# Latent attention with scores formed keys by queries, and row maxima from a separate product

## The chip, the cores and the metric

The kernel runs on one core of one Trainium2 chip. The metric is the device time of one execution in microseconds (us). It is one decoder layer on 1024 tokens with 1024 features; inputs, weights and output are float32.

## What is computed

Each layer normalizes the residual, projects it, and runs two attention branches whose gated sum is projected back; an MLP and an embedding step follow. The change is in branch B, the multi-head latent attention: 8 heads, a 64-wide part without position and a 32-wide rotary part in query and key, values 64 wide, causal.

```python
def _mla_attention(q, k, v):   # q, k (B,S,8,64+32); v (B,S,8,64)
    logits = jnp.einsum('bqhd,bshd->bhqs', qb, k).astype(jnp.float32) * scale
    logits = jnp.where(causal, logits, -jnp.inf)
    probs = jax.nn.softmax(logits, axis=-1).astype(v.dtype)
    o = jnp.einsum('bhqs,bshd->bqhd', probs, v)
```

## The kernel before, in words

The program is written by hand for five instruction streams: `pe` (TensorE), `dve` (VectorE), `act` (ScalarE), `pool` (GpSimd) and `sp` (a DMA queue). Each runs its own list in order, and they meet only in semaphores. Most matmuls take operands that were split into a high part and a low part of type fp32r, and sum three products (high by high, high by low, low by high). A few take plain float32.

After the gate projections (which end at about 388 us) comes a preparation for branch B: `q_nope` and the key products (L2423) fill PSUM, ScalarE writes the high parts (`qn_hi` L1361, `kn_hi` L1373), VectorE the low parts (`qn_lo` L1824, `kn_lo` L1835), rotates the rotary parts (`rope`, L1806 to L1808, L1830, L1852), and scales the keys by their inverse norm (`kn`, L1857). The inverse norm of a query is applied later, as a factor of the exponential. `latent_values` (L2485) forms the values; their first group is copied by ScalarE (L1377), the second by ScalarE (L1385) and VectorE (L1870).

Attention is a list `STEPS` of 64 steps, 32 of branch B, then 32 of branch A. A step is a tile of 128 queries (number i) and a pair p of heads (e = 0, 1). The two heads of a pair lie on partitions 0 to 63 and 64 to 127, so their two score matmuls use different rows of TensorE's array. Steps alternate long and short tiles. In step n of branch B:

- `scores_b(n)` (L2507 and L2511): for each chunk of up to 512 keys, five terms for both heads, the 128 queries as stationary operand and the keys as moving one. Result: queries on partitions, keys along the row, in banks 4 to 7.
- VectorE subtracts the causal mask and takes each row's maximum in one instruction (L1921), scales it (L1923), and raises `shift_ready`. `scores_b(n+1)` waits for it.
- ScalarE applies the exponential with that shift and sums each row at the same time (L1430).
- `turn_probs` (L2544): TensorE transposes each 128x128 tile of the probabilities into a ring of three banks, and ScalarE (L1394) and VectorE (L1882) copy it to SBUF.
- `sum_values` (L2558): float32 matmuls, the values as stationary operand of 64 columns, 128 queries moving, both heads of the pair in different columns of the array. ScalarE copies the result (L1413).

The row sums of branch B are inverted, transposed and spread over partitions during branch A (`invert_sums`, `turn_inverse`, `spread_inverse`, `scale_y`, L1886 to L1899). ScalarE and VectorE split the keys and queries of branch A (L1435, L1933, L1439, L1938) at fixed steps. GpSimd forms low parts of weights (`lo_parts`, L1037) and is otherwise idle in branch B. Branch A (`scores_a`, L2528) has the same pipeline, with a mask of its own; then come the output projections (L2282 and others), the MLP (L2677, L2718) and the rest.

## Time and profile before

| what | value |
|---|---|
| median of 3 runs | 1649.94 us (1649.73 to 1650.37) |
| the profiled execution, its own time | 1650.06 us |
| its span (first to last instruction) | 1648.3 us |
| TensorE's mean granted clock | 0.996 |
| TensorE busy | 1596.7 us (97%) |
| VectorE, ScalarE, GpSimd busy | 1201.2, 699.9, 637.1 us |

Times in the profile count from the start of the span. The busy time is the union of the instructions of an engine; the number in parentheses is the share of the span. PE is TensorE's matmuls and PEld its weight loads. DVE is VectorE, ACT is ScalarE, POOL is GpSimd. A matmul's duration is longer than the distance to the next one, since they overlap; so costs of TensorE are read from the starts.

### The profile page before, as it was taken

Reading aid. Unit: us, or ns where it says so; the run is one execution under the profiler, and the core shown is the slowest. Engines: PE = TensorE matmul, PEld = TensorE weight load, DVE = VectorE, ACT = ScalarE, POOL = GpSimd, SP = SyncE. Lnnn points to the kernel's source line nnn. Section 1 sums busy time; section 2 is a strip of 40 time slices with the busy share of each in tenths; the row PEclk is TensorE's granted clock in tenths of the full one; section 3 lists DMA queues with packets and bytes.
Section 4 is the critical chain, followed back from the end, with each engine's and each line's share of the span. In section 5 each row is a group of like instructions: output and inputs, shape, how many; then the busy total and the mean of one; then the engine's idle time right before and its main releaser. Section 6 shows DMA issues by size and latency. Waiting matters only on the chain.

```text
span 1648.3 us, 23187 instructions
## 1 busy us (share of the span) xinstructions
PE 1596.7 (97%) x8576; PEld 1296.1 (79%) x8576; DVE 1201.2 (73%) x1851; ACT 699.9 (42%) x1151; POOL 637.1 (39%) x397
## 2 busy tenths in 40 slices
PE   6999999999999999999999999999999999999997
PEld 5778888787777777778888788888878888888786
DVE  7679999982656677754354777776699999898445
ACT  5432422323566677621144443343354444444223
POOL 2222532213200002012213545445589888885230
PEclk9999999999999999999999999999999999999999
DMA  5312223243300010203442354555494544422112
GB/s 164 93 39 58 96 77 102 90 126 82 90 1 2 1 40 2 78 25 131 168 137 89 119 169 141 160 171 160 155 338 170 204 163 166 141 90 64 45 58 102
DMA packets 115240, 177.46 MB, mean 108 GB/s; under 512 B 19104, under 2 KB 73376, under 8 KB 115008
## 3 DMA queue, kind: packets, MB, share of 16 engines
q1 hardware_dynamic: 111296, 162.44, 30.2%
q10 hardware_dynamic: 3680, 13.63, 2.2%
q8 instruction: 64, 1.05, 0.3%
q14 instruction: 40, 0.33, 0.1%
q0 software_dynamic: 160, 0.02, 0.0%
HBM read 123.24 MB, written 49.68 MB: 105 GB/s over the span
## 4 chain that ended last, share of the span: by engine, by line
PE 87%; DVE 7%; ACT 3%; issue 2%; POOL 1%; DMA 1%; SPq 0%; ACTq 0%; DVEq 0%
PE ps L2282 35%; PE ps L2718 18%; PE ps L2677 17%; PE ps L2544 3%; PE ps L2558 2%; PE ps L2507 2%; PE ps L2528 2%; PE ps L2423 2%; DVE prob_a L1921 1%; PE ps L2362 1%; PE ps L2330 1%; DVE prob_b L1921 1%; PE ps L2511 1%; PE ps L2641 1%; PE ps L2384 1%
## 5 line engine op out<-in xcount | busy, mean ns | idle before, releaser
L1037 POOL TENSOR_TENSOR w_lo<-w_raw,w_hi 128x1024 fp32r<-128x1024 f32 x67 | 166.1, 2480 | 481.9 <-ACT w_hi L1187 481.9
L1106 POOL TENSOR_TENSOR a_lo<-s_raw,a_hi 128x512 fp32r<-128x512 f32 x128 | 189.8, 1490 | 95.2 <-ACT a_hi L1466 94.8
L1187 ACT ACTIVATE w_hi<-w_raw 128x1024 fp32r<-128x1024 f32 x67 | 70.9, 1059 | 343.0 <-PE ps L2282 275.3
L2677 PE MATMUL ps<-b_hi,a_hi 128*128 128x512 f32 x448 | 175.3, 391 | 3.7 <-POOL a_lo L1106 1.7
L2718 PE MATMUL ps<-b_hi,a_hi 128*128 128x512 f32 x448 | 174.5, 390 | 2.4 <-DVE h L2155 2.4
L2677 PE MATMUL ps<-b_hi,a_lo 128*128 128x512 f32 x448 | 174.4, 389 | 0.0
L2677 PE MATMUL ps<-b_lo,a_hi 128*128 128x512 f32 x448 | 174.3, 389 | 0.0
L1106 POOL TENSOR_TENSOR a_lo<-f_raw,a_hi 128x512 fp32r<-128x512 f32 x96 | 136.8, 1439 | 97.1 <-ACT a_hi L1466 97.0
L2718 PE MATMUL ps<-b_lo,a_hi 128*128 128x512 f32 x448 | 174.3, 389 | 0.0
L2718 PE MATMUL ps<-b_hi,a_lo 128*128 128x512 f32 x448 | 174.3, 389 | 0.0
L2282 PE MATMUL ps<-n_hi,w_hi 128*128 128x512 f32 x544 | 168.3, 391 | 2.4 <-ACT rel L1247 1.3
L1769 DVE TENSOR_SCALAR_CACHE_REDUCE tested<-sc,bar_i 128x384 bf16<-128x384 f32 (+2 forms) x192 | 169.0, 942 | 1.7 <-POOL sc L1052 0.6
L2282 PE MATMUL ps<-n_hi,w_lo 128*128 128x512 f32 x544 | 167.5, 389 | 0.0
L2282 PE MATMUL ps<-n_lo,w_hi 128*128 128x512 f32 x544 | 167.4, 389 | 0.0
L2155 DVE TENSOR_TENSOR h<-h,ps 128x512 f32<-128x512 f32 x224 | 142.8, 677 | 23.4 <-PE ps L2718 23.0
L2105 DVE TENSOR_TENSOR b_lo<-b_lo,b_hi 128x512 fp32r<-128x512 f32 x112 | 143.5, 1321 | 0.1
L2282 PEld LDWEIGHTS ps<-n_hi,w_hi 128*128 128x128 f32 x544 | 101.8, 188 | 25.2 <-ACT rel L1247 1.7
L2282 PEld LDWEIGHTS ps<-n_lo,w_hi 128*128 128x128 f32 x544 | 102.1, 188 | 21.2
L2282 PEld LDWEIGHTS ps<-n_hi,w_lo 128*128 128x128 f32 x544 | 102.1, 188 | 21.2
L1466 ACT ACTIVATE a_hi<-s_raw 128x512 fp32r<-128x512 f32 x128 | 78.7, 627 | 92.5 <-PE ps L2718 90.9
L2677 PEld LDWEIGHTS ps<-b_hi,a_hi 128*128 128x128 f32 x448 | 84.1, 188 | 23.3 <-POOL a_lo L1106 3.3
L2718 PEld LDWEIGHTS ps<-b_hi,a_hi 128*128 128x128 f32 x448 | 84.1, 188 | 21.0 <-issue 3.5
(356 smaller groups left out, 3224.4 us busy)
## 6 DMA issues: line engine op xcount, KB each, us to landing
f_raw<-in_w_ff_dram SPq DMA_DIRECT2D x64, 512.0 KB, 4.3
b_lo<-hid_scratch SPq DMA_DIRECT2D x112, 256.0 KB, 5.5
hid_scratch<-c_out SPq DMA_DIRECT2D x32, 512.0 KB, 3.7
w_raw<-in_w_in_dram SPq DMA_DIRECT2D x28, 512.0 KB, 3.7
hid_scratch<-t_out SPq DMA_DIRECT2D x15, 768.0 KB, 6.1
...
```

What stands on the lines that cost most here:

```text
L1037: pool.tensor_tensor(lo_of(first)[:, :, :], w_raw[s][:, :, :], hi_of(first)[:, :, :].bitcast(F32), ALU.subtract).then_inc(lo_ready, 1)
L1106: pool.tensor_tensor(slot(a_lo, o), first_of(o), slot(a_hi, o).bitcast(F32), ALU.subtract).then_inc(a_lo_done, 1)
L1187: act.activation(hi_of(first)[:, :, :], w_raw[s][:, :, :], ACT.Copy).then_inc(hi_ready, 1)
L1466: act.activation(slot(a_hi, o), first_of(o), ACT.Copy).then_inc(a_hi_done, 1)
L1769: ins = dve.tensor_scalar(tested[:, at0:at0 + KEYS[i]], s_i, bar_f[:, f:f + 1], None, ALU.is_ge, ALU.add, accum_out=count_c[:, f:f + 1])
L1921: link(dve.tensor_tensor_reduce(prob_of(n, e)[:, 0:w], s, less, 1.0, LOWEST, ALU.subtract, ALU.max, top))
L2105: dve.tensor_tensor(b_lo[r][:, b, :], b_lo[r][:, b, :].bitcast(F32), b_hi[r][:, b, :].bitcast(F32), ALU.subtract).then_inc(hid_lo_done, 1)
L2155: dve.tensor_tensor(h[k][:, part], h[k][:, part], pair_bank(w, name, ab), ALU.add).then_inc(added, 1)
L2282: last = pe.matmul(bank(4 * half + 2 * j + t)[0:w, :], wm, xm[:, t * HALF:(t + 1) * HALF], start=(n == 0 and a), stop=(n == total - 1 and ...
L2544: last = pe.transpose(bank(u % RING)[:, (k - k0) * P:(k - k0 + 1) * P], prob_of(n, e)[:, k * P:(k + 1) * P], ident[:, :])
L2677: last = pe.matmul(unit_bank(u, PLACE[name]), w[o % NS][:, j, :], x[j][:, b, :], start=name in ("P1", "P2", "P5") and j == 0 and a, stop=j ...
L2718: last = pe.matmul(pair_bank(w, name, ab), x[(LAST + o) % NS][:, 2 * j + ab, :], y[r][:, b, :], start=name in ("P1", "P2", "P5") and j == ...
```

## The change

Branch B is laid out anew; branch A keeps its steps. The work of branch B is now 8 jobs, each a pair of heads by 512 queries, and 48 units, each one tile of 128 keys of a job.

- `scores_b(u)`: keys stationary (128), up to 512 queries moving, five terms for both heads. On diagonal tiles two more pairs of matmuls (`place_r` by `mask_t`, 128 and 64 columns) add the causal mask. The shift is inside the product: `kr_lo` has a row of ones (a row that was unused), and `q_rope_max` has the negated row maximum in that row.
- The maxima come from `max_scores(m)`, 48 pieces of 128 queries by up to 512 keys, with two terms (high by high, and the rotary part) instead of five. The first six go to banks 4 to 7 by turns, all later ones to banks 0 and 1. VectorE's `take_piece` subtracts the mask on the diagonal block and takes the maximum of both heads (for rows with two pieces, a third instruction joins them). `turn_max(j)` transposes the four maxima tiles of a job into bank 2, and `subtract_max(j)` makes `q_rope_max`.
- ScalarE applies the exponential to both heads of a unit in one instruction, with no row sum. The result is already keys by queries, so there are no transposes and no copies. `values_b(u)` has 512 queries moving.
- Row sums: GpSimd adds each unit's probabilities to the job's first (`add_probs`, 40 instructions of up to 128x1024); a matmul with ones (`sum_probs`) sums over partitions and spreads, VectorE inverts a 128x512 block from PSUM and scales y (`scale_y_b`), once per job.
- The query's inverse norm is now applied before the split: the rotary tables and the query products are multiplied by it on VectorE (`scale_queries`), so the low parts are formed from SBUF (`queries_lo`). A second reciprocal (128x1024) and two products with the tables are added ahead of it, and two memsets of one row in `kr_lo`.
- The second half of `q_rope`'s DMAs waits for all key and query scalings; the transfers are the same. GpSimd builds `mask_t` and `place_r` once; its last two `lo_parts` stand after the additions.
- Order on TensorE: `latent_values(1)` is done token tile by token tile with the first four pieces before each; then 24 rounds g of two units, as the last excerpt shows. `turn_max` of jobs 1 to 7 stands at the end of rounds 0, 2, 4, 8, 10, 14, 18, `sum_probs` of jobs 0 to 6 at the end of rounds 3, 5, 9, 11, 15, 17, 21.
- VectorE's order: pieces of unit u; at even u after a `sum_probs`, `scale_y_b`; at odd u, `subtract_max`; `ka_lo` at u = 20, `qa_lo` at u = 30.

```diff
+        JOBS = [(0, 0), (1, 0), (0, 1), (2, 0), (1, 1), (3, 0), (2, 1), (3, 1)]
+        UNITS_B = [(j, k) for j, (_, c) in enumerate(JOBS) for k in range(4 * (c + 1))]
+        NU = len(UNITS_B)
+        FIRST_B = [UNITS_B.index((j, 0)) for j in range(len(JOBS))]
+        LAST_B = [f - 1 for f in FIRST_B[1:]] + [NU - 1]
+        PIECES = [(j, t, k0, min(HALF, KEYS[4 * c + t] - k0)) for j, (_, c) in enumerate(JOBS) for t in range(4)
+                  for k0 in range(0, KEYS[4 * c + t], HALF)]
+        EARLY = 6
+        PIECES_AT = [range(EARLY + 2 * u, EARLY + 2 * u + 2) if u < 5 else range(u + 11, u + 12) for u in range(NU)]
+        PIECES_AT = [[m for m in r if m < len(PIECES)] for r in PIECES_AT]
+        LAST_PIECE = [max(m for m, piece in enumerate(PIECES) if piece[0] == j) for j in range(len(JOBS))]
+        TURN_AT = [-1] + [(1 + next(u for u, ms in enumerate(PIECES_AT) if LAST_PIECE[j] in ms)) // 2
+                          for j in range(1, len(JOBS))]
+        SUM_AT = [(u + 1) // 2 + 1 for u in LAST_B]
...
+        def taken(m):
+
+            return m + 1 + sum(1 for x in JOINED if x < m)
+
+        def rows_taken(j):
+
+            m = LAST_PIECE[j]
+            return taken(m) + (m in JOINED)
...
                                pattern=[[-1, P]], channel_multiplier=1).then_inc(mask_ready, 1)
-            lo_parts(HEADS - 1)
+            pool.memset(max_rows_both[:, :], 0.0).then_inc(mask_ready, 1)
+            lo_parts(HEADS - 3)
+
...
+            def add_probs(u):
+                j, lo = UNITS_B[u][0], lo_of_unit(u)
+                total = first_b[j % 2][:, :, lo:HALF]
+                pool.wait_ge(prob_ready, u + 1)
+                pool.wait_ge(pv_done, FIRST_B[j] + 1)
+                if adds_before(u):
+                    pool.wait_ge(sums_added, adds_before(u))
+                pool.tensor_tensor(total, total, probs_of(u)[:, :, lo:HALF], ALU.add).then_inc(sums_added, 1)
+
...
+            for u in ADDS:
+                add_probs(u)
+            pool.wait_ge(y_norm, len(JOBS))
+            lo_parts(2)
 
             for k in range(YT):
...
+            def exponents(u):
+                j, k = UNITS_B[u]
+                act.wait_ge(s_ready[0], u + 1)
+                act.wait_ge(s_ready[1], u + 1)
+                if k == 0:
+                    if j >= 2:
+                        act.wait_ge(sum_done, j - 1)
+                elif adds_before(u) >= 4:
+                    before = ADDS[adds_before(u) - 4]
+                    act.wait_ge(pv_done, before + 1)
+                    act.wait_ge(sums_added, adds_before(u) - 3)
+                act.activation(probs_of(u)[:, :, lo_of_unit(u):HALF], score_banks(u), ACT.Exp).then_inc(prob_ready, 1)
...
+            def scale_queries(g):
+                half = group(2)
                 for j in range(2):
-                    wait_hi(dve, "qn", 2 * g + j)
-                    last = dve.tensor_tensor(qn_lo[:, 2 * g + j, :], tile_ps(half, j),
-                                             qn_hi[:, 2 * g + j, :].bitcast(F32), ALU.subtract)
-                last.then_inc(psum_free[half], 1)
...
             rope(qr[:, 1, :], tile_ps(half, 1))
             dve.sem_inc(psum_free[half], 1)
+            queries_lo(0)
             rope_lo(0)
-            half, _, _, _ = at_.group(2)
-            queries_lo(1, half)
...
+            def take_piece(m):
+                j, t, k0, w = PIECES[m]
+                _, c = JOBS[j]
+                b = piece_bank(m)
+                dve.wait_ge(max_ready, m + 1)
+                if k0 + w == KEYS[4 * c + t]:
+                    own = ps[:, b:b + 2, w - P:w]
+                    link(dve.tensor_tensor(own, own, mask[:, :].unsqueeze(1).to_broadcast([P, 2, P]), ALU.subtract))
+                at0 = t * MAX_PITCH + ROPE
+                row = max_rows[j % 2][:, at0:at0 + HEAD_DIM + 1:HEAD_DIM]
+                if j >= 2 and m in JOINED + [x for x in range(len(PIECES)) if JOBS[PIECES[x][0]][1] == 0]:
+                    dve.wait_ge(max_turned, j - 1)
+                at1 = 4 * (t % 2)
+                top = row if c == 0 else halves_c[:, at1 + 2:at1 + 4] if k0 else halves_c[:, at1:at1 + 2]
+                dve.tensor_reduce(top, ps[:, b:b + 2, 0:w], AXIS.X, ALU.max).then_inc(max_taken, 1)
+                if k0:
+                    dve.wait_ge(max_taken, taken(m))
+                    dve.tensor_tensor(row, halves_c[:, at1:at1 + 2], halves_c[:, at1 + 2:at1 + 4], ALU.max).then_inc(max_taken, 1)
+
+            def subtract_max(j):
+                p, c = JOBS[j]
+                dve.wait_ge(max_turned, j + 1)
+                if j == 0:
+                    dve.wait_ge(q_moved, ROPE_MOVED[0])
+                if j >= 2:
+                    dve.wait_ge(s_ready[1], LAST_B[j - 2] + 1)
+                dve.tensor_tensor(q_rope_max[j % 2][:, :], q_rope[p][:, c * HALF:(c + 1) * HALF].bitcast(F32),
+                                  bank(AUX_BANK), ALU.subtract).then_inc(shift_ready, 1)
+
             def copy_turned(n):
...
+            def scale_y_b(j):
+                p, c = JOBS[j]
+                dve.wait_ge(sum_done, j + 1)
+                dve.reciprocal(inv_b[:, :], sum_bank(j)).then_inc(sum_inverted, 1)
+                dve.wait_ge(sum_inverted, j + 1)
+                dve.wait_ge(y_copied, j + 1)
+                y = yb[:, p, c * HALF:(c + 1) * HALF]
+                dve.tensor_tensor(y, y, inv_b[:, :], ALU.mult).then_inc(y_norm, 1)
...
+            for u in range(NU):
+                for m in PIECES_AT[u]:
+                    take_piece(m)
+                if u % 2 == 0 and u // 2 - 1 in SUM_AT:
+                    scale_y_b(SUM_AT.index(u // 2 - 1))
+                if u % 2 and u // 2 in TURN_AT:
+                    subtract_max(TURN_AT.index(u // 2))
...
+            def max_scores(m):
+                j, t, k0, w = PIECES[m]
+                p, c = JOBS[j]
+                q, keys, b = slice((4 * c + t) * P, (4 * c + t + 1) * P), slice(k0, k0 + w), piece_bank(m)
+                before = m - 2 if m < EARLY else m - 1
+                if before >= 0:
+                    pe.wait_ge(max_taken, taken(before))
+                if k0 == 0 and t == 0 and j < PAIRS:
+                    wait_hi(pe, "kn", [x for x, _ in JOBS[:j + 1]][-1])
+                if (p, j) in ((2, 3),):
+                    pe.wait_ge(q_moved, ROPE_MOVED[1])
+                for x, y, a in ((qn_hi[:, p, :], kn_hi[:, p, :], True), (q_rope[p], kr_hi, False)):
+                    for e in range(2):
+                        r = slice(e * HEAD_DIM, (e + 1) * HEAD_DIM)
+                        last = pe.matmul(bank(b + e)[:, 0:w], x[r, q], y[r, keys], start=a, stop=not a)
+                last.then_inc(max_ready, 1)
...
+            def turn_max(j):
+                pe.wait_ge(max_taken, rows_taken(j))
+                if j:
+                    pe.wait_ge(shift_ready, j)
+                inverted = sum(1 for g in SUM_AT if g < TURN_AT[j])
+                if inverted:
+                    pe.wait_ge(sum_inverted, inverted)
+                for t in range(4):
+                    last = pe.transpose(bank(AUX_BANK)[:, t * P:(t + 1) * P],
+                                        max_rows[j % 2][:, t * MAX_PITCH:t * MAX_PITCH + P], ident[:, :])
+                last.then_inc(max_turned, 1)
...
+            def scores_b(u):
+                j, k = UNITS_B[u]
+                p, c = JOBS[j]
+                lo, b = lo_of_unit(u), 4 + 2 * (u % 2)
+                keys, q = slice(k * P, (k + 1) * P), slice(c * HALF + lo, (c + 1) * HALF)
+                if u < 2:
+                    pe.wait_ge(max_taken, taken(EARLY - 1))
+                else:
+                    pe.wait_ge(prob_ready, u - 1)
+                terms = [(kn_hi[:, p, :], qn_hi[:, p, q]), (kn_lo[:, p, :], qn_hi[:, p, q]), (kn_hi[:, p, :], qn_lo[:, p, q]),
+                         (kr_hi, q_rope[p][:, q]), (kr_lo, q_rope_max[j % 2][:, lo:HALF])]
+                for t, (y, x) in enumerate(terms):
+                    if t == 1 and u == 0:
+                        wait_lo(pe, "kn", HEADS // 2 - 1)
+                    if t == 4 and k == 0:
+                        pe.wait_ge(shift_ready, j + 1)
+                    if t == 4 and on_diagonal(u):
+                        if u == 0:
+                            pe.wait_ge(mask_ready, 6)
+                        for first, q0, n in ((HEAD_DIM, HEAD_DIM, HEAD_DIM), (0, 0, P)):
+                            for e in range(2):
+                                r = slice(e * HEAD_DIM, (e + 1) * HEAD_DIM)
+                                pe.matmul(bank(b + e)[:, lo:lo + n], place_r[r, first:first + P], mask_t[r, q0:q0 + n],
+                                          start=False, stop=False)
+                    for e in range(2):
+                        r = slice(e * HEAD_DIM, (e + 1) * HEAD_DIM)
+                        last = pe.matmul(bank(b + e)[:, lo:HALF], y[r, keys], x[r, :], start=t == 0, stop=t == 4)
+                        if t == 4:
+                            last.then_inc(s_ready[e], 1)
...
+            def values_b(u):
+                j, k = UNITS_B[u]
+                p, lo = JOBS[j][0], lo_of_unit(u)
+                pe.wait_ge(prob_ready, u + 1)
+                if k == 0 and j:
+                    pe.wait_ge(y_copied, j)
+                for e in range(2):
+                    last = pe.matmul(bank(Y_BANK)[e * HEAD_DIM:(e + 1) * HEAD_DIM, lo:HALF],
+                                     vb[:, k, (2 * p + e) * HEAD_DIM:(2 * p + e + 1) * HEAD_DIM], probs_of(u)[:, e, lo:HALF],
+                                     start=k == 0, stop=u in LAST_B)
+                last.then_inc(pv_done, 1)
+
+            def sum_probs(j):
+                pe.wait_ge(sums_added, adds_before(LAST_B[j] + 1))
+                pe.wait_ge(shift_ready, sum(1 for g in TURN_AT if g <= SUM_AT[j]))
+                if j:
+                    pe.wait_ge(sum_inverted, j)
+                if j == len(JOBS) - 1:
+                    pe.wait_ge(y_copied, len(JOBS))
+                for e in range(2):
+                    last = pe.matmul(sum_bank(j)[e * HEAD_DIM:(e + 1) * HEAD_DIM, :], ones[:, 0:HEAD_DIM],
+                                     first_b[j % 2][:, e, :], start=True, stop=True)
+                last.then_inc(sum_done, 1)
...
+            for g in range(NU // 2):
+                for m in PIECES_AT[2 * g]:
+                    max_scores(m)
+                scores_b(2 * g)
+                scores_b(2 * g + 1)
+                for m in PIECES_AT[2 * g + 1]:
+                    max_scores(m)
+                if g:
+                    values_b(2 * g - 2)
+                    values_b(2 * g - 1)
+                if g in TURN_AT:
+                    turn_max(TURN_AT.index(g))
+                if g in SUM_AT:
+                    sum_probs(SUM_AT.index(g))
+            scores_a(0)
+            for u in range(NU - 2, NU):
+                values_b(u)
+
             for n in range(1, N + 2):
-                if n == 4:
-                    pe.wait_ge(q_moved, ROPE_MOVED[1])
```

## Rows read from the trace of the kernel before

**Rows 1.** The page: busy time, and the chain of waits by engine.

```profile
PE 1596.7 (97%) x8576; PEld 1296.1 (79%) x8576; DVE 1201.2 (73%) x1851; ACT 699.9 (42%) x1151; POOL 637.1 (39%) x397
...
PE 87%; DVE 7%; ACT 3%; issue 2%; POOL 1%; DMA 1%; SPq 0%; ACTq 0%; DVEq 0%
```

**Rows 2.** Windows, branch B and branch A: us, busy of each engine, granted clock, DMA.

```profile
433.00:578.00 145.00, 135.56 (x1326) 106.94 (x1326) 83.80 (x242) 94.45 (x212) 4.70 (x2) 0.98 0.07 18
578.00:705.00 127.00, 119.73 (x1215) 92.02 (x1215) 90.72 (x262) 90.86 (x225) 9.86 (x5) 1.00 0.12 38
```

**Rows 3.** The chain in order of time: start, duration, piece of the chain.

```profile
436.03 5.75 PE ps L2485 x24
...
576.43 2.05 PE ps L2544 x16
578.85 1.18 PE ps L2528 x11
...
916.29 1.72 PE ps L2653 x4
```

**Rows 4.** Timeline of TensorE and VectorE in branch B: start, duration.

```profile
535.17 0.41 PE L2511 MATMUL ps<-kr_lo,q_rope 64*128 64x512 f32 x2
...
535.39 0.35 PE L2507 MATMUL ps<-kn_hi,qn_hi 64*128 64x384 f32 x2
535.57 0.35 PE L2507 MATMUL ps<-kn_lo,qn_hi 64*128 64x384 f32 x2
...
544.64 0.39 PE L2511 MATMUL ps<-kr_lo,q_rope 64*128 64x512 f32 x2
...
545.07 1.23 DVE L1921 CUSTOM_DVE_ANT_0 prob_b<-ps,mask 128x1024 f32<-128x1024 f32 x1 [2.45 <-PE ps L2511]
...
545.55 1.75 PE L2558 MATMUL ps<-prob_tb,vb 128*64 128x128 f32 x28
```

**Rows 5.** Groups by shape: VectorE's and TensorE's instructions, count, busy, mean ns.

```profile
L2558 PE MATMUL ps<-prob_tb,vb 128*64 128x128 f32 x576 | 38.9, 280 | 0.0
...
L1882 DVE COPY prob_tb<-ps 128x512 f32<-128x512 f32 x11 | 7.5, 685 | 1.2 <-PE ps L2544 1.2
L1882 DVE COPY prob_tb<-ps 128x256 f32<-128x256 f32 x12 | 4.9, 416 | 0.4 <-PE ps L2544 0.4
...
L1802 DVE RECIPROCAL rms_c<-rms_c 128x1024 f32<-128x1024 f32 x1 | 6.5, 6543 | 0.0
```

**Rows 6.** Groups by shape: GpSimd's additions of 128x1024.

```profile
L1069 POOL TENSOR_TENSOR rms_c<-rms_c,stage 128x1024 f32<-128x1024 f32 x3 | 7.3, 2424 | 0.0
L1161 POOL TENSOR_TENSOR sq_sum<-sq_sum,h_squares 128x1024 f32<-128x1024 f32 x2 | 6.6, 3295 | 0.1
```

**Rows 7.** Timeline of the preparation, 388 to 434 us.

```profile
388.88 0.29 DVE L1817 COPY perm<-ident 128x64 f32<-128x64 f32 x2 [12.95 <-DMA gates_scratch<-stage]
...
409.01 1.22 DVE L1808 TENSOR_TENSOR qr<-qr,rope_t 128x1024 f32<-128x1024 f32 x1
...
412.35 2.65 POOL L1037 TENSOR_TENSOR w_lo<-w_raw,w_hi 128x1024 fp32r<-128x1024 f32 x1 [6.70 <-ACT w_hi L1187]
...
412.78 3.30 DVE L1808 TENSOR_TENSOR qr<-qr,rope_t 128x1024 f32<-128x1024 f32 x1
...
422.66 2.36 DVE L1857 TENSOR_TENSOR kn<-ps,rms_c 128x1024 f32<-128x1024 f32 x2 [0.84 <-PE ps L2423]
...
433.56 2.42 ACT L1377 ACTIVATE vb<-ps,cols 128x512 f32<-128x512 f32 x4 [2.07 <-PE ps L2485]
```

**Rows 8.** Windows around a long wait of TensorE, columns as in rows 2.

```profile
478.00:480.00 2.00, 0.91 (x12) 0.77 (x14) 1.66 (x1) 0.95 (x3) 0.00 (x0) 1.00 0.00 0
480.00:482.00 2.00, 1.12 (x11) 0.57 (x7) 1.93 (x8) 0.61 (x1) 0.00 (x0) 0.78 0.00 0
...
486.00:488.00 2.00, 2.00 (x16) 1.67 (x16) 1.93 (x7) 1.38 (x3) 0.00 (x0) 0.51 0.00 0
```

420 lines of the change are left out of this document (236 added, 184 removed).

## The prediction

> **What bounds the kernel now.** First the page: TensorE is busy 97% of the span and holds 87% of the chain that ends last [rows 1]. So the change is worth what it does to TensorE's own time or to its waits. Then the windows of the two branches: branch B takes 145 us, with TensorE busy 135.6, VectorE 83.8, ScalarE 94.5 and GpSimd 4.7 [rows 2]. The chain in order of time shows where branch B ends: the first scores of branch A start at 578.85 [rows 3]. All terms below are summed against that moment. Durations come from the profiled execution, whose 1650.06 us are 0.1 above the median; I forecast against the median.
>
> **TensorE's work, before.** Costs are distances between starts. A pair of score matmuls (both heads) of 512 columns takes 0.23, of 384 0.175 [rows 4]; for 256 I take half of 512, 0.12, and for 128 hardly less, 0.11, since each pair needs its two weight loads. The 5 terms over 24, 8, 8, 8 chunks of these widths give 5 x (24 x 0.23 + 8 x 0.175 + 8 x 0.12 + 8 x 0.11) = 43.8 us. Transposes: 16 in 2.05 us [rows 3], 288 of them, 36.9. Values: 576 records for 288 float32 matmuls [rows 5], so a matmul has two; 28 records in 1.75 us [rows 4] is 0.125 a matmul, 36. Second half of the latent values 5.75 [rows 3]. Sum 122.5, and the window also holds idle and half-clock time.
>
> **TensorE's work, after.** Scores: the same chunks and terms, 43.8. Mask: 32 diagonal units by two short pairs, 32 x 0.22 = 7.0 added. Maxima: two terms of the same chunks, 43.8 x 2/5 = 17.5 added. Transposes: -36.9, and 32 for the maxima, +4.1. Values: a pair with 512 columns costs at most four pairs with 128, 4 x 0.25 = 1.0. Below it is bounded by the two full-width float32 matmuls of 512 columns in 1.72 us [rows 3], 0.86 each. I take 0.87, since that row has the same length of columns: 24 x 0.87 + 8 x 0.65 + 8 x 0.44 + 8 x 0.22 = 31.4, down 4.6. Sums: 8 pairs of 512 float32 columns, 8 x 0.87 = 7.0 added. So 122.5 becomes 116.6: TensorE saves 6 us and no more. Each change of kind of work (piece, scores, piece, values) costs about 0.1 (the first of the transposes after the last score pair comes that much late in the same timeline), 4 x 24 rounds, 9.6 us.
>
> **What moves ahead of the first scores.** VectorE gets new work in the preparation. The second reciprocal (6.5) [rows 5] and two table products (2 x 1.22) lie in an idle stretch of 12.95 us [rows 7], so they cost nothing; without that cover they'd cost 9. Scaling the queries adds 4 x 1.2 = 4.8 us later, and it frees the first PSUM group 1.1 us earlier than `qn_lo` did. Two one-row memsets add 0.1 to 1.2 each; I take 0.6. VectorE is back to back from 409 to 421, and the keys' scaling waited only 0.84 for TensorE [rows 7]; so it moves from 422.7 to about 427.5, and `latent_values(0)`, which needs that PSUM, from 427.6 to about 430. The copies of its result on ScalarE (2.42 at 433.56 [rows 7]) come after the last `kn_hi`, which is late by 4: they end near 439.5. Before, 2.4 us of scores stood in that gap; now one piece of 0.2 does. The second latent group then runs from 439.6 to 446.7 (5.75, three pieces with 1.05, switches). VectorE then has two value copies, pieces 4 and 5 and the first `subtract_max`, to 451.3. TensorE has piece 6 at 450.6 and cannot place piece 7 before piece 6 is read, 452.9. First scores: 453.5. GpSimd builds the masks from 446.7 on, ten short instructions, about 3 us, so they are there in time.
>
> From there TensorE has the loop: 43.8 + 7.0 + 17.5 + 31.4 + 4.1 + 7.0 = 110.8, less 3.0 that is done, plus 9.6 of switches: 117.4. With no wait the scores of branch A would start at 571, which is **8 us earlier** than before.
>
> **VectorE and the single buffer.** This is where I expect the time to go. After the sixth piece all pieces use banks 0 and 1, so TensorE cannot issue one before VectorE has read the last. A 128x512 read from PSUM costs 0.685, 128x256 0.416, 128x1024 1.23 [rows 4, 5]: a piece costs 1.22 off the diagonal, and with mask (0.42 and a gap of 0.1) 0.94, 1.21, 1.47, 1.74 for 128 to 512 keys; the join adds 0.3. The way from the last matmul to VectorE takes 0.43 [rows 4]. So from piece to piece pass about 0.76 + 1.22 + 0.1 = 2.1, up to 2.9 us.
> - Rounds 0 to 3 have up to four pieces each, two of them back to back. TensorE has 19.3 us of work there; walked piece by piece they take 27.5 (453.5 to 481). **+8**.
> - From round 4 on a round is piece, scores (2.3), piece, values (1.74 or less). That covers a piece, but not a `scale_y_b`: the reciprocal of 128x512 is half of 6.54, 3.3 us [rows 5], the product after it 0.7 to 1.3. In round 6: the diagonal piece is read 2.1 us in, `scale_y_b` ends at 6.4, the second piece is read at 7.7, and TensorE has work for 5.0. Wait 2.8. The same at rounds 12 and 16 (2.8, 4.0); at 4, 10 and 18 `turn_max` needs bank 2, which the reciprocal still reads, and waits 2.1, 2.1, 1.3, then 1.7 once more for the next piece at 4 and 10. Sum 18.5, with small ones 19.5, less 1.5 for switches that these waits hide. **+18**.
> - `ka_lo` (2.3) at u = 20 and `qa_lo` (1.2) at u = 30 stand on VectorE between two pieces, the first just behind a `scale_y_b`. **+4**.
>
> **GpSimd's additions.** 40 of them, 28672 columns. At 2.42 us for 1024 [rows 6] that is 68, with fixed parts 74 us, beside 150: no wait, and at 3.3 [rows 6] 92, still none. If a job's seven (14 us) did not fit between its first values and its sum, the sum would wait; the rounds between take 18. But they disturb VectorE. A product that started at 412.78 beside a running GpSimd operation took 3.30, the same line alone 1.22, and it ended 1.1 after GpSimd's [rows 7]. The 16 joins, the products with `inv_b` and the two low parts have both inputs in SBUF like it. Bounds: 0 to 2.4 us each, for the 16 joins 0 to 38; I take half an operation at a share of 0.6, 0.7 each, and of the 11 us some 4 reach TensorE past the slack of the scores. **+4** (0 to 15).
> The Trainium skill ("SBUF — State Buffer", Who interferes with whom) says that a VectorE operation with two SBUF inputs and a GpSimd operation that reads SBUF block each other for the whole instruction, and that one with a PSUM input does not; the trace agrees on the 3.30.
>
> **The clock.** In branch B it fell once: TensorE was busy 2.0 of 4 us, then the granted clock was 0.5 (1.2 GHz) for about 7 us [rows 8], which costs 3.5. The waits in the preparation and in rounds 0 to 3 are as long, but there VectorE is the limit and a slow TensorE hides in part. **+3** (0 to 20).
> The Trainium skill ("TensorE: Matmul & The Clock Gate", HAM oscillation) warns that bursts with waits between them drop the clock each time.
>
> **ScalarE and branch A.** ScalarE loses the copies and row sums and has 48 exponentials of 1.05 or less: never the limit. Branch A loses two inverse transposes' groups and four spreads (3 us of TensorE, 8 x 0.68 of VectorE), but its pipeline now starts empty (scores, maximum, exponential with nothing beside them, about 3). **0** (-4 to +5). The moved DMAs of `q_rope` are needed only by job 3: 0.
>
> Sum: -8 + 8 + 18 + 4 + 4 + 3 = +29: 1650 + 29 = **1679 us**.
>
> **The rivals.**
> 1. *VectorE stays hidden* (chance 0.13): the pieces and reciprocals fit beside TensorE, because the low parts of the preparation come sooner or the waits overlap. For it: VectorE has about 105 us of work in 150. Against: the buffer is single, and the long block stands between two pieces. It decides if a `scale_y_b` costs under 1.5 us or so, where round 6 has no wait. Then only -8 + 4 remains: 1646, and 1642 at best.
> 2. *The clock drops at each long wait* (0.17): eight more waits of 2 us and over, each like the one at 480; 6 of them x 3.5 = +21: 1700. For it: the one wait of that size did it. Against: branch A has many short waits at full clock [rows 2].
> 3. *GpSimd is the limit* (0.07): its operations stretch to 3.3 or more beside VectorE, the ring of four buffers fills, and exponentials wait. Some 2 us in each of the 4 long jobs, +8: 1687.
> 4. *The waits are half of it* (0.18), because reads and matmuls overlap more than I allowed: +15: 1665.
>
> The forecast keeps 0.45. The range 1650 to 1700 leaves out the better half of rival 1 and the far end of rival 2. A measurement here can tell 0.2%, 3.3 us. Faster by that: 0.1 (rival 1); within: 0.04; slower: 0.86.
>
> **What would show it.** Right: first keys-by-queries scores at about 453; rounds 0 to 3 with VectorE near full and TensorE near 70%; VectorE's reciprocals of 3.3 us with TensorE idle behind them; the first scores of branch A between 600 and 612; joins far over 0.2 us. Wrong: TensorE over 95% busy through the loop and branch A before 580; or a granted clock of 0.5 in most rounds; or a value pair of 512 columns at twice 0.87, which would add 25.

## The result, and the profile after

The changed kernel takes **1694.03 us** (median of 4 runs, 1693.11 to 1695.07) against 1650.15 for the kernel before beside it (1649.73 to 1650.66): ratio 1.0266, 95% interval 1.0248 to 1.0284. It is 44 us slower. The forecast was 1679, range 1650 to 1700: the sign and the range held, and 15 us are missing from the sum. The profiled execution took 1694.82 us, its span is 1692.9.

The page of the changed kernel, busy times, the chain by engine, and the group of the new additions:

```profile
PE 1611.2 (95%) x8256; PEld 1285.3 (76%) x8256; DVE 1244.1 (73%) x1729; ACT 654.9 (39%) x996; POOL 707.2 (42%) x446
...
PE 83%; DVE 9%; ACT 3%; issue 2%; POOL 1%; DMA 1%; SPq 0%; ACTq 0%; POOLq 0%; DVEq 0%
...
L1157 POOL TENSOR_TENSOR first_b<-first_b,prob_b 128x1024 f32<-128x1024 f32 (+3 forms) x40 | 70.0, 1751 | 103.8 <-PE ps L2726 88.3
```

Beside [rows 1]: TensorE has 320 instructions fewer and is busy 14.5 us *longer*, and its mean granted clock over the span fell from 0.996 to 0.978. VectorE's share of the chain rises from 7 to 9%.

In the timeline of the changed kernel the first weights of the keys-by-queries scores are loaded at 457.7, their first matmul starts at 458.2 (forecast 453.5), and the first scores of branch A, L2759, start at 622.4, where before they stood at 578.85 [rows 3]. That is 43.5 of the 44; branch A itself, from there to the first matmul of the output projections, takes 128.1 us against 127.0. So nearly everything is in the preparation and in the 164.7 us of branch B's loop. The windows of that stretch, changed kernel; us, then busy of TensorE, its weight loads, VectorE, ScalarE and GpSimd, granted clock, DMA share, GB/s:

```profile
457.00:480.00 23.00, 18.33 (x100) 11.95 (x100) 9.99 (x17) 3.99 (x5) 2.20 (x2) 0.58 0.00 1
480.00:520.00 40.00, 31.22 (x258) 21.33 (x260) 28.02 (x31) 10.93 (x14) 18.62 (x12) 0.92 0.00 1
520.00:560.00 40.00, 31.43 (x228) 19.59 (x224) 26.57 (x28) 11.52 (x13) 13.94 (x9) 0.86 0.00 1
560.00:600.00 40.00, 35.34 (x256) 22.84 (x256) 24.28 (x30) 11.76 (x15) 14.03 (x9) 0.83 0.00 1
600.00:622.00 22.00, 20.24 (x174) 12.34 (x172) 8.69 (x5) 8.39 (x11) 16.02 (x9) 1.00 0.01 1
```

These five lines give the account of the loop. TensorE is busy 136.6 of 165 us. Busy time times granted clock, line by line, is 10.6 + 28.7 + 27.0 + 29.3 + 20.2 = 116 us (to the rounding): the work at full clock, which the forecast had counted as 117.4 with its switches. The clock takes 136.6 - 116 = 20.6, and 28.4 are idle. The clock 0.58 is mostly its lower level, 1.2 of 2.4 GHz; ahead of it and in it TensorE issued short pieces with waits of 1.2 to 2.1 us between them. The waits of TensorE from 450 to 625, changed kernel (us in total, times, longest):

```profile
PE ps L2674 <- DVE cols L2008: 23.3, 11, 4.9
PE ps L2685 <- DVE inv_b L2055: 5.0, 3, 1.8
PE ps L2674 <- DVE max_rows_both L2008: 2.7, 2, 1.5
```

L2674 is `max_scores`, which waits for VectorE to read the previous piece; L2685 is `turn_max`, which waits for the reciprocal to release bank 2. The two waits of the third row end at 455.0 and 457.2, ahead of the loop; the 23.3 and 5.0 of the others make up all its 28 us of idle time. The longest of them, on VectorE's timeline of the changed kernel, and then its end on TensorE's:

```profile
505.38 0.69 DVE L2008 TENSOR_REDUCE cols<-ps 128x2 f32<-128x512 f32 x1
506.11 1.70 DVE L2011 TENSOR_TENSOR max_rows_both<-cols 128x2 f32<-128x2 f32 x1
507.73 3.35 DVE L2055 RECIPROCAL inv_b<-ps 128x512 f32<-128x512 f32 x1
511.11 2.26 DVE L2059 TENSOR_TENSOR yb<-yb,inv_b 128x512 f32<-128x512 f32 x1
513.29 1.21 DVE L2008 TENSOR_REDUCE cols<-ps 128x2 f32<-128x1024 f32 x1
...
514.56 0.69 PE L2674 MATMUL ps<-kn_hi,qn_hi 64*128 64x384 f32 x2 [4.87 <-DVE cols L2008]
```

Between two pieces VectorE has 7.3 us of other work: a join (1.70, where another takes 0.16), the reciprocal, the product (2.26 where another takes 0.69). The next piece is issued at 507.2 and done by 507.8, so it stands finished in banks 0 and 1 for 5.5 us before VectorE reads it. VectorE's groups by shape, 430 to 640, changed kernel (count, busy, mean ns, idle before):

```profile
L2055 DVE RECIPROCAL inv_b<-ps 128x512 f32<-128x512 f32 x8 | 26.8, 3347 | 9.8 <-PE ps L2739 9.8
L2008 DVE TENSOR_REDUCE cols<-ps 128x2 f32<-128x1024 f32 x20 | 24.4, 1221 | 23.6 <-PE ps L2674 23.5
L2001 DVE TENSOR_TENSOR ps<-ps,mask 128x256 f32<-128x256 f32 x32 | 13.8, 431 | 32.7 <-PE ps L2674 32.5
L2059 DVE TENSOR_TENSOR yb<-yb,inv_b 128x512 f32<-128x512 f32 x8 | 10.3, 1282 | 0.3
L2011 DVE TENSOR_TENSOR max_rows_both<-cols 128x2 f32<-128x2 f32 x16 | 6.5, 408 | 0.6
```

And VectorE's waits from 450 to 625, the same stretch as TensorE's above:

```profile
DVE ps L2001 <- PE ps L2674: 27.5, 22, 3.1
DVE cols L2008 <- PE ps L2674: 23.5, 10, 3.9
```

TensorE waits 26 us for VectorE's reads, and VectorE waits 51 us for TensorE's pieces. Neither is full; with one buffer they take turns. That holds for rounds 0 to 3 too, which end with the first `sum_probs` at 490.9 (columns as in the windows above):

```profile
457.70:490.90 33.20, 27.52 (x198) 18.32 (x194) 16.80 (x26) 7.40 (x10) 5.13 (x4) 0.72 0.00 0
```

### The profile page after: what moved, and what is told of

The parts are those of the page before. It is cut to its first block, busy times and chain, and to the rows that moved or that the text cites. A ratio compares the mean times of both kernels' runs of the same rounds, so it can differ in the third digit from the quotient of the medians.

```text
span 1692.9 us, 22200 instructions
## 1 busy us (share of the span) xinstructions
PE 1611.2 (95%) x8256; PEld 1285.3 (76%) x8256; DVE 1244.1 (73%) x1729; ACT 654.9 (39%) x996; POOL 707.2 (42%) x446
## 4 chain that ended last, share of the span: by engine, by line
PE 83%; DVE 9%; ACT 3%; issue 2%; POOL 1%; DMA 1%; SPq 0%; ACTq 0%; POOLq 0%; DVEq 0%
PE ps L2449 33%; PE ps L2973 17%; PE ps L2932 16%; PE ps L2715 2%; PE ps L2759 2%; PE ps L2674 2%; PE ps L2779 1%; DVE inv_b L2055 1%; DVE prob_a L2096 1%; PE ps L2497 1%; PE ps L2726 1%; PE ps L2529 1%; DVE cols L2008 1%; PE ps L2794 1%; PE ps L2896 1%
## 5 line engine op out<-in xcount | busy, mean ns | idle before, releaser
L1092 POOL TENSOR_TENSOR w_lo<-w_raw,w_hi 128x1024 fp32r<-128x1024 f32 x67 | 164.7, 2458 | 464.3 <-ACT w_hi L1272 457.1
L1157 POOL TENSOR_TENSOR first_b<-first_b,prob_b 128x1024 f32<-128x1024 f32 (+3 forms) x40 | 70.0, 1751 | 103.8 <-PE ps L2726 88.3
L2932 PEld LDWEIGHTS ps<-b_hi,a_hi 128*128 128x128 f32 x448 | 84.2, 188 | 23.3 <-POOL a_lo L1191 3.3
```

Source lines behind the costliest of these rows:

```text
L1092: pool.tensor_tensor(lo_of(first)[:, :, :], w_raw[s][:, :, :], hi_of(first)[:, :, :].bitcast(F32), ALU.subtract).then_inc(lo_ready, 1)
L1157: pool.tensor_tensor(total, total, probs_of(u)[:, :, lo:HALF], ALU.add).then_inc(sums_added, 1)
L2932: last = pe.matmul(unit_bank(u, PLACE[name]), w[o % NS][:, j, :], x[j][:, b, :], start=name in ("P1", "P2", "P5") and j == 0 and a, stop=j ...
```

## The experiments

Theory V is that of the forecast: one buffer of pieces, read behind a long block on VectorE. Its rivals are the clock (rival 2 of the forecast) and GpSimd's additions (rival 3, or their effect on VectorE). All differences are against 1694.03; every run's ratio is to the kernel before beside it, whose median stayed between 1649.75 and 1650.5. Runs 1, 2, 4, 5, 6 and 7 were timed twice each, so a difference of 2 or 3 us between them says little. "A starts" is the first scores of branch A.

**1 to 3. Take the long block away, then the piece's reading, then both.** In the first the row sums are copied instead of inverted, so branch B is multiplied by its sums. In the second the maxima are read from the first 128 keys of a piece alone (and the exponent scaled by 0.125), so the maxima are others. The third does both.

```
-dve.reciprocal(inv_b[:, :], sum_bank(j)).then_inc(sum_inverted, 1)
+dve.tensor_copy(inv_b[:, :], sum_bank(j)).then_inc(sum_inverted, 1)
...
-dve.tensor_reduce(top, ps[:, b:b + 2, 0:w], AXIS.X, ALU.max).then_inc(max_taken, 1)
+dve.tensor_reduce(top, ps[:, b:b + 2, 0:P], AXIS.X, ALU.max).then_inc(max_taken, 1)
```

> VectorE's reciprocal of each job's 128x512 sums (3.35 us, eight times) is replaced by a copy (about 0.69); y comes out scaled by the sum and not by its inverse. All else as in the changed kernel (1694). Theory V (one buffer for the pieces, and a long VectorE block between two of them): the waits of TensorE of 1.6 at the turns in rounds 4 and 10, 4.9 in round 7, 3.3 in round 11 and the like in rounds 13, 17, 18 shrink by 2.66 each at most, and with them drops of the clock; 16 to 25 us less, 1669 to 1678. Rival C (the loss is the half clock, set off by the preparation and by the short maxima products, whatever the reciprocal does): under 8 us less, above 1686.

Measured: 1673.74, ratio 1.0138 (1.0109 to 1.0168); A starts at 602.6. So -20.3. Its windows (columns as above):

```profile
457.00:480.00 23.00, 18.29 (x100) 12.01 (x100) 10.07 (x16) 3.99 (x5) 1.93 (x2) 0.57 0.00 1
480.00:520.00 40.00, 36.18 (x298) 23.73 (x296) 26.25 (x34) 11.55 (x15) 19.23 (x12) 0.91 0.00 1
520.00:560.00 40.00, 34.15 (x277) 21.87 (x277) 25.70 (x32) 13.47 (x17) 17.36 (x10) 0.91 0.00 1
560.00:602.00 42.00, 41.10 (x346) 25.22 (x344) 19.30 (x25) 17.59 (x23) 26.13 (x14) 1.00 0.01 1
```

TensorE is busy 129.7 of 145 us, and busy time times granted clock is 10.4 + 32.9 + 31.1 + 41.1 = 115.5. So the idle time fell from 28.4 to 15.3, and what the clock takes from 20.6 to 14.2: of the gain some 13 are waits and 6 to 7 the clock.

> Each piece's maximum reads only the first 128 keys of each head, 0.43 us in place of up to 1.22; the maxima are then too small for long rows, so the exponential also gets a factor of 0.125 to stay finite (same instruction, same time). Theory V: the waits between two pieces of one round in rounds 0 to 3 and the tail of each long block go, 0.8 us for each of the 24 pieces of 512 keys that TensorE waits for; some 12 to 20 us less, 1674 to 1682, most of it before round 4. Rival C: TensorE's work in those rounds is the same and stays at half clock; under 6 us less.

Measured: 1683.44, ratio 1.0197 (1.0168 to 1.0227); A starts at 610.0. So -10.6.

> Both together: copy for reciprocal, and 128-key maxima (exponential with a factor of 0.125). VectorE then fits in everywhere. If TensorE's own work is what I summed (117 us from the first scores on) and its clock stays up, branch A starts near 573 to 580 against 622, and the time is 1645 to 1655. If rounds on TensorE cost more than I counted (value pairs, switches, exponentials not ready), it stays above 1660; the loop's length then says by how much.

Measured: 1655.76, ratio 1.003 (1.0016 to 1.0044, 8 runs); A starts at 588.3. So -38.3, more than 20.3 and 10.6 together. The 8 executions fall into two groups, 1652.8 to 1654.0 with a mean granted clock of 0.992 or 0.993 and 1657.5 to 1658.1 with 0.989; the median lies between them, and the profiled one took 1658.1. Its windows (columns as above):

```profile
457.00:480.00 23.00, 20.51 (x132) 14.11 (x132) 7.23 (x19) 4.68 (x6) 3.81 (x3) 0.66 0.00 1
480.00:520.00 40.00, 38.43 (x348) 25.17 (x348) 21.35 (x40) 13.56 (x19) 20.44 (x12) 1.00 0.01 1
520.00:560.00 40.00, 35.59 (x314) 23.20 (x310) 23.05 (x38) 17.14 (x21) 18.58 (x12) 1.00 0.00 1
560.00:588.00 28.00, 28.00 (x228) 16.23 (x224) 8.05 (x9) 11.15 (x14) 22.18 (x11) 1.00 0.01 1
```

What follows: nearly all of the 44 us goes through VectorE's two jobs between the pieces, the reciprocal's part being the larger. And the work at full clock is again 13.5 + 38.4 + 35.6 + 28.0 = 115.5 us, so TensorE's own count is right and the rest is waits and clock. With this little on VectorE the kernel is still 0.3% behind the kernel before: A starts at 588.3, 9.5 later than before, since the loop starts late and its first 23 us still run at 0.66 (7 us lost).

**4. Keep the clock without shortening a wait.** Unused score products stand where TensorE would wait: after the first piece, between back-to-back pieces, and in 8 rounds before the piece.

```
+def fill(b, n):
+    for _ in range(n):
+        for e in range(2):
...
+            pe.matmul(bank(b + e), kn_hi[r, 0, 0:P], qn_hi[r, 0, 0:HALF], start=True, stop=True)
+FILL = {1: 5, 2: 5, 3: 4, 5: 5, 7: 14, 11: 10, 13: 14, 17: 16}
```

> Nothing is taken away. Unused score products (pairs of 512 columns into banks that the next scores overwrite) fill TensorE's waits: 5 between the two pieces of a unit in rounds 0 to 2, 4 to 16 at the start of rounds 1, 2, 3, 5, 7, 11, 13, 17, and 9 after the first piece. If the half clock costs real time beyond the waits (rival C, or V with a large clock term), the granted clock stays near 1.00 from 460 to 600 and the time falls by 8 to 18 us, to 1676 to 1686, though TensorE does 20 us more work. If the half clock hides under the waits (as I priced it, 3 us), the time is the same or a few us longer.

Measured: 1680.34, ratio 1.0178 (1.0149 to 1.0208); A starts at 605.1. So -13.7, with more work on TensorE and none less on VectorE. Its windows:

```profile
457.00:480.00 23.00, 19.98 (x187) 14.62 (x186) 15.12 (x22) 6.42 (x8) 3.86 (x3) 0.99 0.01 1
480.00:520.00 40.00, 36.84 (x338) 24.93 (x336) 28.88 (x33) 11.12 (x15) 17.39 (x10) 1.00 0.00 1
520.00:560.00 40.00, 36.04 (x308) 23.48 (x308) 29.78 (x31) 12.21 (x15) 17.40 (x10) 1.00 0.00 1
560.00:605.00 45.00, 42.84 (x350) 26.21 (x348) 24.83 (x22) 16.74 (x21) 26.63 (x14) 1.00 0.01 1
```

The granted clock is 0.99 or 1.00 where it was 0.58, 0.92, 0.86 and 0.83. This is the direct measure of the term that the forecast priced at 3: at least 13.7. It is a lower bound, since the filling has a price too. In its loop (149.2 us) TensorE's own 116 us of work leave 33 for waits and unused products, where the changed kernel had 28 of waits; so the edit cost some 5, and the clock gave back nearly all of its 20.

**5. The keys earlier in the preparation.** On VectorE the keys' scaling and low parts go ahead of the second queries' low parts, `kr_lo` last.

```
-LO_ORDER = [("qn", 0), ("qn", 1), ("qr", 0), ("qn", 2), ("qn", 3), ("qr", 1), ("kr", 0)] + HI_ORDER[8:]
+LO_ORDER = [("qn", 0), ("qn", 1), ("qr", 0), ("qn", 2), ("qn", 3), ("qr", 1)] + HI_ORDER[8:12] + [("kr", 0)] + HI_ORDER[12:]
```

> Only VectorE's order in the preparation changes: the first half of the keys is scaled right after the second half of the queries, the second half before the keys' low parts, and the low part of the rotary key with its two memsets comes last (TensorE waits for it before the last term of the first unit). Same instructions, same output. My account of the preparation (TensorE waited 2.7, 2.1, 2.1 us there for work of VectorE that stood behind later-needed work): the second latent group starts near 436 in place of 442, the first scores near 452 in place of 457.7, 1687 to 1690. Rival (the preparation is VectorE's total, whatever the order): the first scores stay at 456 to 458, 1692 to 1695.

Measured: 1691.72, ratio 1.0253 (1.0231 to 1.0275): -2.3, of two executions of 1689.61 and 1693.84. The second was profiled. In it the first scores come 4.4 earlier (453.8 against 458.2), but A starts only 1.0 earlier (621.4). The lead isn't lost in the first rounds: `sum_probs` of jobs 0 to 5 all start 4.1 to 4.2 earlier, here that of job 5. It goes right after, when the granted clock falls once more, behind a wait of 1.8 us at 597.8. Run 5, and then the changed kernel, where a wait of the same length ends at 601.9 and the clock stays up:

```profile
589.94 1.03 PE L2745 MATMUL ps<-first_b,ones 128*64 128x512 f32 x4
...
600.00:604.00 4.00, 4.00 (x24) 2.05 (x20) 0.51 (x1) 0.98 (x2) 3.58 (x3) 0.50 0.00 0
```

```profile
594.09 1.03 PE L2739 MATMUL ps<-first_b,ones 128*64 128x512 f32 x4
...
600.00:604.00 4.00, 2.24 (x32) 1.95 (x32) 3.97 (x2) 0.33 (x1) 3.66 (x3) 1.00 0.01 4
```

So an earlier start is passed on whole to job 5, and whether an execution keeps it is decided by one more fall of the clock. The faster execution, 4.4 under the changed kernel, fits one that kept it; it has no profile, so that isn't shown.

**6. The inverse on ScalarE**, as exp(-ln(sum)); VectorE only multiplies, one unit later.

```
+act.activation(inv_b[:, :], sum_bank(j), ACT.Ln).then_inc(sum_inverted, 1)
+act.wait_ge(sum_inverted, j + 1)
+act.activation(inv_b[:, :], inv_b[:, :], ACT.Exp, scale=-1.0).then_inc(inv_formed, 1)
```

> The inverse of the sums moves from VectorE (3.35 us) to ScalarE, as a logarithm and an exponential with a factor of -1 (about 0.6 each, and perhaps two table loads of 1.28), which has much idle time; VectorE keeps the product, now behind the next piece. The output stays the reference's. Theory V: nearly all that the run with a copy gave, 16 to 22 us less, 1672 to 1678. Rival: ScalarE's table loads and waits delay the exponentials, units wait for their probabilities, and under half of it comes: above 1684.

Measured: 1684.87, ratio 1.0211 (1.0189 to 1.0233): -9.2, half of what the copy gave. ScalarE's groups in this run, then a wait of VectorE:

```profile
L1519 ACT ACT_TABLE_LOAD x8 | 10.3, 1283 | 0.1
L1521 ACT ACT_TABLE_LOAD x8 | 10.3, 1283 | 0.1
```

```profile
DVE yb L2071 <- ACT inv_b L1521: 24.5, 6, 16.7
DVE ka_lo L2089 <- ACT ka_hi L1538: 6.3, 1, 6.3
PE ps L2727 <- ACT prob_b L1513: 6.4, 6, 1.8
```

Each job costs ScalarE two table loads of 1.28 us, and that comes back in three places. VectorE, which works in order, stands before the product; of the 24.5 us, 16.7 are one wait after the last piece, when TensorE has none left to wait for, and 7.8 in five waits lie among the pieces. ScalarE forms `ka_hi` behind the inverse of job 2, VectorE waits 6.3 us for it in front of `ka_lo`, and TensorE then waits 6.5 us for the next piece's bank, the longest wait of this run. And TensorE, which never waited for probabilities in the changed kernel's loop, now does so for 6.4 us. So this is the rival of this run as much as theory V: the block got another owner, and the owner's other work came later.

**7. Pieces apart.** The second piece of a pair stands between the scores of two units, or between their values.

```
 scores_b(2 * g)
+for m in first[1:]:
+    max_scores(m)
 scores_b(2 * g + 1)
...
     values_b(2 * g - 2)
+for m in second[1:]:
+    max_scores(m)
```

> TensorE's order in rounds 0 to 2 alone: the second of two pieces that stood back to back goes between the two units' scores, and on the other side between the two values. Theory V: a piece then has 1 us or more of other work behind it, so of the waits of 1.3 to 1.5 between pieces in rounds 0 to 3 half goes, and the clock comes back sooner: 4 to 9 us less, 1685 to 1690. Rival (VectorE's total bounds these rounds): under 3 us.

Measured: 1683.44, ratio 1.0203 (1.0181 to 1.0225): -10.6. In the profiled execution the whole preparation ran 2.8 earlier (the keys' scaling at 428.40 against 431.25), and `sum_probs` of job 0, at the end of round 3, 11.1 earlier; so some 8 are the edit's own, all of them made in rounds 0 to 3. The granted clock from 457 to 480 is 0.93 instead of 0.58, while the waits for the reciprocal stay (longest 4.9).

**8. Edits 5, 6 and 7 together.**

> Keys first, inverse on ScalarE and pieces apart together; the output stays the reference's. If the three act at different places their gains add: 5 + 19 + 6 less than 1694, 1660 to 1668, still slower than the kernel before (1650), because TensorE's loop with everything short took 131 us and not 117. If they overlap (each only removes the same half clock), 1670 to 1676.

Measured: 1674.89, ratio 1.0148 (1.013 to 1.0166): -19.1, against 22 for the sum of the single ones.

**9. Filling, pieces apart, and the reciprocal in two halves** of 256 columns with a piece between them.

```
+link(dve.reciprocal(inv_b[:, 0:HALF // 2], sum_bank(j)[:, 0:HALF // 2]))      # where scale_y_b stood
+dve.reciprocal(inv_b[:, HALF // 2:], sum_bank(j)[:, HALF // 2:])              # one unit later, then the product
```

> Three edits at once on the changed kernel: unused score products fill the waits (about half as many per round as in the fill experiment), the second piece of a pair stands between the scores or between the values, and the reciprocal is formed in two halves of 256 columns (1.7 us each) with a piece read between them. Theory (single buffer and clock as two prices that add): filling alone gave 14 us, pieces apart gave 8 of its own; the halves make the longest block on VectorE 1.7 + 2 instead of 5.5, worth up to half of the 20 that skipping the reciprocal gave. Forecast 1671, scores of branch A first at 597. Rival 1 (the waits are now short, so the filling products only cost): 1680 or more. Rival 2 (waits and clock feed each other, together they give more than their sum): below 1665. At or under the kernel before (1650) I expect nothing.

Measured: 1682.82, ratio 1.019 (1.0173 to 1.0207): -11.2, a miss, and no better than pieces apart alone. TensorE's waits in this run:

```profile
PE ps L2691 <- DVE inv_b L2058: 10.8, 3, 5.9
PE ps L2680 <- DVE cols L2008: 6.1, 7, 1.4
```

and VectorE's halves, by shape:

```profile
L2058 DVE RECIPROCAL inv_b<-ps 128x256 f32<-128x256 f32 x8 | 14.0, 1752 | 0.1
L2054 DVE RECIPROCAL inv_b<-ps 128x256 f32<-128x256 f32 x8 | 14.0, 1748 | 13.2 <-PE ps L2751 13.2
```

The pieces now wait 6 us instead of 23, but `turn_max` (L2691) waits 10.8 instead of 5.0: its bank is free only after the second half, which stands one unit later. The wait moved to the other user of the block. The edits were tried together only, so what each gave here stays open.

**10. GpSimd's additions shortened to 128 columns a head**, on top of the copy of run 1. This leaves out most of branch B's row sums.

```
+lo = HALF - P
 total = first_b[j % 2][:, :, lo:HALF]
```

> Beside the run that replaced the reciprocal by a copy (1673.7, waits for the pieces 17.5 us): GpSimd's 40 additions all take 128 columns a head (about 0.75 us) instead of 128 to 512. This leaves out most of the row sums of branch B, so its output is scaled otherwise. Theory (GpSimd's additions cost little: joins and products of VectorE that stand beside them): joins fall from 0.50 to about 0.2, products with the inverse from 1.45 to 0.75, together 10 us of VectorE, of which 4 reach TensorE, and the clock moves with them; 1668 to 1671. Rival 1 (they cost nothing on the path): 1673.7 within 3. Rival 2 (they hold the port for much more than the rows show, 10 us or more on the path): 1663 or less. The scores of branch A should start by 598 with the theory.

Measured: 1662.01, ratio 1.0071 (1.0054 to 1.0088); A starts at 593.2, against 602.6 in run 1. So -11.7 against that run: rival 2 of this run. VectorE's two operations with both inputs in SBUF, in run 1 and then here, 430 to 640:

```profile
L2059 DVE TENSOR_TENSOR yb<-yb,inv_b 128x512 f32<-128x512 f32 x8 | 10.8, 1356 | 0.3
...
L2011 DVE TENSOR_TENSOR max_rows_both<-cols 128x2 f32<-128x2 f32 x16 | 8.1, 504 | 0.6
```

```profile
L2060 DVE TENSOR_TENSOR yb<-yb,inv_b 128x512 f32<-128x512 f32 x8 | 5.6, 698 | 0.3
...
L2012 DVE TENSOR_TENSOR max_rows_both<-cols 128x2 f32<-128x2 f32 x16 | 2.6, 162 | 0.6
```

GpSimd's additions take 10.8 + 8.1 - 5.6 - 2.6 = 10.7 us of VectorE's time by stretching these 24 operations, and about as much comes back on the kernel. A wait of 1.0 us of `sum_probs` for the additions goes too. The clock is part of it: from 480 to 520 it is 1.00 here and 0.91 in run 1, from 520 to 560 0.96 and 0.91. The Trainium skill ("SBUF — State Buffer", Who interferes with whom) says that such operations and a GpSimd operation that reads SBUF block each other for the whole instruction; the trace agrees, down to a join of 128x2 that takes 1.70 us instead of 0.16.

**11. Filling and copy together.**

> The filling products of the fill experiment (1680.3) and the reciprocal replaced by a copy (1673.7) together, so branch B's output is multiplied by the sum instead of its inverse. If clock and waits are two separate prices: 1694 - 13.7 - 20.3 = 1660. If the copy's gain was itself half clock (shorter waits kept the clock), they overlap: 1665 to 1668. If filling costs more than it gives once the long waits are gone: 1670 or more. Granted clock from 480 to 590: 1.00 in every case.

Measured: 1668.52, ratio 1.0108 (1.0091 to 1.0125), at the edge of the overlap that was expected. Filling gives 13.7 with the reciprocal in place and 5.2 without it; the copy gives 20.3 without filling and 11.8 with it. That the two overlap by some 8 us agrees with the 6 to 7 of clock in run 1's windows, but is no clean measure of it: the filling was sized for the long waits, and with the copy TensorE is busy 135.9 of the 140.2 us of the loop, so part of the 8 is unused products where no wait was left.

**12. The inverse by query.** TensorE sums with `first_b` as weights and one column of ones, so a job's sums stand as 128 queries by 8; VectorE inverts 8 columns; TensorE spreads them with the identity; the product reads the spread inverse in PSUM. With edits 5 and 7.

```
+for t in range(4):
+    for e in range(2):
+        pe.matmul(sum_bank(j)[:, 2 * t + e:2 * t + e + 1], first_b[j % 2][:, e, t * P:(t + 1) * P], ones[:, 0:1], ...)
...
+dve.reciprocal(inv_b[:, 0:8], sum_bank(j)[:, 0:8]).then_inc(sum_inverted, 1)
...
+pe.matmul(sum_bank(j)[e * HEAD_DIM:(e + 1) * HEAD_DIM, t * P:(t + 1) * P],
+          inv_b[:, 2 * t + e:2 * t + e + 1].to_broadcast([P, HEAD_DIM]), ident[:, :], ...)
...
+dve.tensor_tensor(y, y, sum_bank(j), ALU.mult).then_inc(y_norm, 1)
```

> The order of the keys' preparation and the pieces apart as in the run of three edits (1674.9), but the inverse formed another way: TensorE sums with the additions' tile as weights and one column of ones, so a job's sums stand as 128 queries by 8; VectorE inverts 8 columns instead of 512; TensorE spreads them again by 8 short products with the identity; VectorE multiplies with the spread inverse still in PSUM, so both its inputs no longer lie in SBUF. Theory (the long block costs 20, the GpSimd part is largely the products beside its additions, 6 of 12): 1694 - 20 - 6 - 8 (pieces apart) - 2 (order) + 8 (TensorE's new products, 1 us a job) = 1666; VectorE's products at 0.69 to 0.75, reciprocals under 0.3. Rival 1 (TensorE's extra work and a new round trip cost more than that): 1672 or more. Rival 2 (clock and waits gain together): 1658 or less. Under the kernel before (1650) would need TensorE without any wait, which I don't expect.

Measured: 1673.30, ratio 1.0139 (1.0122 to 1.0156); A starts at 599.6. So -20.7: rival 1 of this run. VectorE's product and reciprocal by shape, this run, and then TensorE's sums and spread of one job in its timeline:

```profile
L2066 DVE TENSOR_TENSOR yb<-yb,ps 128x512 f32<-128x512 f32 x8 | 5.5, 682 | 4.6 <-PE ps L2760 4.6
...
L2059 DVE RECIPROCAL inv_b<-ps 128x8 f32<-128x8 f32 x8 | 1.7, 207 | 25.0 <-PE ps L2752 25.0
```

```profile
514.39 1.95 PE L2752 MATMUL ps<-ones,first_b 128*128 128x1 f32 x16
...
516.93 1.09 PE L2760 MATMUL ps<-ident,inv_b 128*64 128x128 f32 x16
```

VectorE's side did what was wanted: 26.8 us of reciprocals became 1.7, and the product takes 0.68 in every case, beside GpSimd too. But TensorE pays 1.95 + 1.09 a job for what was one group of 1.0, so 2 us a job and 16 in all, where 8 were expected: a product with a single column takes 0.24, more than the 0.14 of one with 128 columns and weights half as wide. Which part of it sets that time isn't shown. It is the fastest version that still computes all of branch B (run 8's interval overlaps with it), and the kernel before stays 1.4% ahead of it.

## Why the prediction was right, and where it was short

- **TensorE's work: right.** 117.4 counted, 116 in the windows; 115.5 in run 3. A value pair of 512 columns takes 0.86 to 0.91 (0.87 taken), a job's sums 1.0 (0.87). Each is the distance to the next start.
- **First scores: 4.2 late**, as is the piece ahead of them (457.15, forecast 452.9). The keys' scaling began at 431.25, not 427.5. A `qn_lo` pair took 4.54 us instead of 2.4 since a GpSimd operation stood beside it, the same case as the 3.30 of [rows 7], and the two memsets took 0.91 each with gaps of 0.25, where 0.6 stood for each. In run 5 a start 4.4 earlier was passed on whole to job 5, so the delay counts in full.
- **The waits for VectorE: right as a sum.** +8, +18, +4 and +4 made 34 us; the rows show 28.3 us of such waits in the loop, all of its idle time. In rounds 0 to 3 they are 5.7 (8 taken), after them 22.6. `turn_max` waited 3 times, 1.6 to 1.8 us (2.1, 2.1 and 1.3 worked out); the three long waits for a piece behind a `scale_y_b` were 4.9, 4.9 and 3.1 (2.8, 2.8 and 4.0 worked out), and the one behind `ka_lo` 3.3. Runs 1 to 3 show that reciprocals and pieces are the cause: without both, 38 of 44 are gone.
- **The clock: the step that failed.** "+3 (0 to 20)" was the price of one stall, on the ground that in rounds 0 to 3 VectorE is the limit and a slow TensorE hides in part. The sign that it named for this, VectorE near full and TensorE near 70%, did not come: VectorE is busy 16.8 of 33.2 us there (51%) and TensorE 27.5 (83%), and the rounds took 33.2 where 27.5 were expected. Measured: 20.6 us of TensorE's time in the loop, 7.7 of them in rounds 0 to 3 (27.52 busy at 0.72), and 13.7 come back when only the clock is kept (run 4). After round 3 the clock fell to 0.50 four times, after each of the four waits of 3 us and more, and took 13 us, 3.3 each; the forecast's row gave 3.5. So rival 2 had mechanism and unit price right, and its number wrong (6 falls, not 4); that its +21 meets the 20.6 is luck, since it priced waits of 2 us and over, and 7.7 of the 20.6 fell in rounds 0 to 3, where no wait was longer than 1.3. The two causes are not rivals but act together: run 3 gives 38.3 where runs 1 and 2 give 30.9 in sum. The rule of the Trainium skill that the prediction cited ("TensorE: Matmul & The Clock Gate", HAM oscillation) warned of this, and the trace agrees with it: the granted clock is 0.58 to 0.92 in the windows with such waits, and 0.99 or 1.00 where run 4 fills them.
- **GpSimd: right in kind, the size low at the path.** The joins cost 6.5 - 16 x 0.16 = 3.9 us and the products 10.3 - 8 x 0.69 = 4.8 beyond their own time, 8.7 together. The 11 of the forecast are the 16 joins at 0.7 alone; the products and low parts that it names beside them are not in its sum, so that 8.7 lies near 11 is partly luck. The forecast let 4 of 11 reach TensorE; run 10 shows 11.7 on the kernel, though beside the copy, where joins and products were stretched more (10.7). Alone, with the reciprocal in place, it wasn't tried. Rival 3 is out: the exponentials waited 0.2 us in all for GpSimd's additions.
- **Branch A: right.** +1 against 0. GpSimd's last seven additions end at 627.7, behind branch A's first scores, and cost the last sum 1.2 us.

By the windows, then: 4.2 of start, -5.6 of waits (28.4 against 34), -1.4 of work, +17.6 of clock is 14.8 us. Branch A started 14.5 later than the 607.9 (578.85 + 29) that the sum gave; the windows begin 0.7 ahead of the loop and end 0.4 before it does. The start and the clock are over, the waits and the work under, and the range held with 6 us to spare.

No run gave the pieces a second buffer, and none moved `scale_y_b` unchanged to another place in VectorE's order. That shorter blocks between two reads help is shown; that a second buffer would is only argued.
